# Alternating the two column ranges of 768-column products inside each k-tile

## The chip, the cores and the metric

One Trainium2 chip, and one of its NeuronCores. The metric is the device time of one execution in microseconds; below a time is a median of several runs unless it is called the profiled execution, which is one run with the hardware profiler on.

## What is computed

Two blocks of a small diffusion-like network in float32, with d = 1024, 256 context tokens and 512 latent tokens. The first block has a hybrid layer and an attention layer, each followed by an MLP; the second has two gated layers on the latent tokens alone.

```python
hx = rms_norm(x, norm1_g[layer]) * (1 + mod_x[1]) + mod_x[0]
hc = rms_norm(s_c, norm1_g[layer]) * (1 + mod_c[1]) + mod_c[0]
y_c, y_x = hybrid_mixer(hc, hx, ...)        # layer 0: projections (h @ w_in), mLSTM, gated conv, @ w_out
...                                         # layer 1: attention_mixer
x = x + mod_x[2] * y_x
x = x + mod_x[5] * sqrelu_mlp(rms_norm(x, ...) * (1 + mod_x[4]) + mod_x[3], mlp_w1[layer], mlp_w2[layer])
# layer 0 does the same for the context tokens s_c
```

All large products have the form weights times activations, with activations held transposed: channels on the 128 partitions, tokens along the free dimension. In layer 0 and in the keys and values of layer 1 the weights apply to context and latent tokens together, 256 + 512 = 768 columns. Everything later is on the 512 latent columns.

## The kernel before

Weights come in units of 1024 x 128 (512 KB), one for each tile of 128 output channels. SyncE loads unit t into slot t % 4 of Wraw, ScalarE copies it to Whi in float32r, and VectorE makes Wlo = Wraw - Whi. Activations too are kept as a high and a low part (h_hi, h_lo; hid_hi, hid_lo; mixa, mixb, mixc in the same way). A product is then the sum of three matmul passes for each k-tile of 128 input channels: Whi with hi, Whi with lo, Wlo with hi. KD = 8 k-tiles make one output tile, accumulated in PSUM.

`product(t, src, rng, ...)` (lines 547 to 563) computes one output tile. It waits for w_lo (the split weights) and for tile_free of its PSUM tensor, issues all passes, and counts tile_done with its last pass. `parts(rng)` (line 335) cuts the token range: FULL, 768 columns, gives (0, 256) and (256, 768); LAT, the 512 latent columns, gives one part. `ps(G[t % 2], a, b)` is where a part goes in PSUM: columns 256 to 512 of G for the 256-column part and 512 to 1024 for the other, thus two banks of 512 floats. G[0] and G[1] alternate from tile to tile, so that ScalarE and VectorE read one tile while TensorE writes the next; both wait for tile_done before they read either part.

Every `pe.matmul` is two instructions on the chip: LDWEIGHTS puts 128 weight columns into the array (PEld in the profile) and MATMUL streams 256 or 512 columns of activations past them (PE).

`product` is used with FULL by the hybrid layer's projections (units 2 to 24), by its output projection (4 tiles), by the MLP of layer 0 and by two tiles of the attention's keys and values; with LAT by everything behind that. The first two tiles of a group are made by others. `first_products` (line 565) runs two tiles at once, a k-tile of one and then a k-tile of the other a few behind, with all three passes of 256 and then all three of 512 in each (lines 587 to 589). `full_part` (line 742 to 744) and `part_product` (654 to 656) make one part of a tile at the seams between groups, where a norm is still being computed for the other part.

Line numbers are those of the kernel before.

Of the kernel before, what the change touches and what calls it, by code (L numbers as in the profile page):

```python
# [14 lines left out]
P = 128  # L15
# [84 lines left out]
def wait(eng, sem, at):  # L100

    if not isinstance(at, At):
        at = At(at)
    if at.positive():
        eng.wait_ge(sem, at.value())


def build(nc, xin, cvec, wstream, adaw, firstw, vecs_d, consts_d, rope_d, poolw_d, sguw_d, rows_d, out):
    ctx = ExitStack()
    with ctx:  # L110
        def sb(name, shape, dt=F32, where=ctx):
            return where.enter_context(nc.sbuf_tensor(name, shape, dt))
# [13 lines left out]
        Wlo = sb("Wlo", [P, 4, D], F32R)  # L126
        Whi = sb("Whi", [P, 4, D], F32R)
# [141 lines left out]
        G = [ctx.enter_context(nc.psum_tensor(f"G{i}", [P, 1024], F32)) for i in range(2)]  # L269
# [8 lines left out]
        def ps(bank, a, b):  # L278

            return bank[:, NC + a:NC + b]  # L280
# [54 lines left out]
        def parts(rng):  # L335
            return [(0, NC), (NC, NT)] if rng == FULL else [(NC, NT)]
# [73 lines left out]
        def is_apart(t):  # L410

            return t.i is None and t.c in APART

        def w_of(t):

            if is_apart(t):
                n = APART[t.c][0]
                return Eraw[:, n, :], Ehi[:, n, :], Elo[:, n, :]
            return Wraw[:, t % 4, :], Whi[:, t % 4, :], Wlo[:, t % 4, :]
# [126 lines left out]
        def _(pe):  # L546
            def product(t, src, rng, kt=KD, from_group=False):

                wait(pe, w_lo, t + 1)
                wait(pe, tile_free[t % 2], t // 2 + (-1 if from_group else 0))  # L550
                s = t % 4
                for a, b in parts(rng):
                    for k in range(kt):
                        hi, lo = src(k)
                        if is_apart(t):
                            wh, wl = [w[:, k * P:(k + 1) * P] for w in w_of(t)[1:]]
                        else:
                            wh, wl = Whi[:, s, k * P:(k + 1) * P], Wlo[:, s, k * P:(k + 1) * P]
                        o = ps(G[t % 2], a, b)
                        pe.matmul(o, wh, hi[:, a:b], start=(k == 0), stop=False)  # L560
                        pe.matmul(o, wh, lo[:, a:b], start=False, stop=False)  # L561
                        last = pe.matmul(o, wl, hi[:, a:b], start=False, stop=(k == kt - 1))  # L562
                last.then_inc(tile_done, 1)

            def first_products(t, src, rng, sem, at, kt=KD, between=None, order=None, lag=None):
# [27 lines left out]
            def tiles(pair):  # L593

                return lambda k: (pair[0][:, k, :], pair[1][:, k, :])

            def latent(pair):

                class Shifted:
                    def __init__(self, ap):  # L600
                        self.ap = ap

                    def __getitem__(self, key):
                        return self.ap[:, key[1].start - NC:key[1].stop - NC]

                return lambda k: (Shifted(pair[0][:, k, :]), Shifted(pair[1][:, k, :]))
# [204 lines left out]
            def mlp(t0, h, hid, rng, sset, h0_, edge):  # L811
                src = tiles(h) if rng == FULL else latent(h)
                hsrc = tiles(hid) if rng == FULL else latent(hid)

                def chunk(i, c0):
                    u0, g0 = t0 + 2 * CH * c0, h0_ + CH * c0
                    if c0 == 0 and rng == FULL:
                        full_start(edge, u0, src)
                    elif c0 == 0:
                        edge_start(edge, u0, src, sset)  # L820
                    else:
                        first_products(At(u0, i, 2 * CH), src, rng, src_ready, At(8 * sset))
                    group = c0 == 0 and rng == LAT
                    for j in range(4 if group else 2, CH):
                        product(At(u0 + j, i, 2 * CH), src, rng, from_group=group and j < 6)
                    first_products(At(u0 + CH, i, 2 * CH), hsrc, rng, hid_ready, At(g0, i, CH))
                    split = rng == FULL and c0 == n - 1
                    for m in range(2, KD - 2 if split else KD):
                        product(At(u0 + CH + m, i, 2 * CH), hsrc, rng)
                    if split:  # L830
                        full_end(edge + 1, u0 + 2 * CH - 2, hsrc)

                n = HID // P // CH
                chunk(None, 0)
                with pe.Fori(0, n - 2 if rng == FULL else n - 1) as i:
                    chunk(i, 1)
                if rng == FULL:
                    chunk(None, n - 1)
# [35 lines left out]
            src = tiles(h0)  # L874
# [99 lines left out]
            for t in range(2, N_HYB):  # L974
                product(At(t), src, FULL)
                if t == 5:
                    gate_columns()
                if 6 <= t < 10:
                    turn(t - 6, 0, TT)
                if t == 7:  # L980
                    turn_keys(0)
                if t in (8, 9):
                    chunk_states(0, t - 8)
                if t in S_SLOT:
                    scores(S_SLOT.index(t))
                if t in A_SLOT:
                    spread_max(A_SLOT.index(t))
                if t in C_SLOT:
                    numerators(C_SLOT.index(t))
                if t == 12:  # L990
                    turn_keys(1)
                if t in (15, 16):
                    chunk_states(1, t - 15)
                if t >= 22:
                    turn_head(t - 22)
# [17 lines left out]
            src = tiles(h2)  # L1013
# [33 lines left out]
            for t in range(N_ATT):  # L1047
                rng = FULL if t < 4 else LAT
# [90 lines left out]
            src = latent(ao)  # L1139
# [6 lines left out]
            for l in range(2):  # L1146
                t0 = T_S + l * N_S
                src = latent(hs)
# [50 lines left out]
                src = latent(ms)  # L1199
# [5 lines left out]
                src, hsrc = latent(hs), latent(hid2)  # L1205

                for c0, n_up in ((0, CH), (1, CH), (2, NF - 2 * CH)):
                    t = t1 + 24 * c0
# [1836 lines left out]
```

## Time and profile before

| | |
|---|---|
| median of 3 runs | 2559.99 us |
| lowest and highest | 2555.70 and 2561.22 us |
| profiled execution, its own time | 2557.46 us |
| its span, first to last instruction | 2555.80 us |
| PE busy in the span | 2512.2 us, 98% |
| PEld busy | 2120.1 us, 83% |
| VectorE (DVE), ScalarE (ACT) busy | 1617.5 us, 63%; 970.0 us, 38% |
| mean granted TensorE clock | 0.993 of full |

The span is what the profile's rows cover. Busy time is a union over the instructions of an engine; the ends of matmuls are modelled, and successive ones overlap, so that the start of one to the start of the next is shorter than its duration.

### The profile page before, as it was taken

How to read it: one execution, taken by the hardware profiler on the slowest of the kernel's cores; microseconds unless marked ns; L12 is line 12 of the kernel's file. 1: busy time of each engine (PE TensorE's matmuls, PEld its weight loads, DVE VectorE, ACT ScalarE, POOL GpSimd, SP SyncE). 2: the span in 40 equal slices, each digit the busy share in tenths (PEclk: the TensorE clock that was granted, in tenths of full speed). 3: DMA queues.
4: the chain of work that ended last, by engine and by line, in shares of the span. 5: the costliest groups of instructions: out<-in, count | busy, mean ns of one | idle time of the engine just before them, and what ended most of it. 6: DMA issues, size and time to landing. Idle time of an engine off the chain costs nothing.

```text
span 2555.8 us, 36124 instructions
## 1 busy us (share of the span) xinstructions
PE 2512.2 (98%) x13956; PEld 2120.1 (83%) x13956; DVE 1617.5 (63%) x2547; ACT 970.0 (38%) x1440; POOL 93.8 (4%) x181
## 2 busy tenths in 40 slices
PE   8999999999999999999999999999999999999997
PEld 6888888888888886669888888888888888888887
DVE  5777666764646556666655566776667867744447
ACT  6243533131313244764332243453232454533234
POOL 0000000000000000000000000000001000000000
PEclk9999999999999999999999999999999999999998
DMA  7323413433333311002545553324456323132322
GB/s 284 109 98 100 140 50 132 165 116 116 115 107 130 110 67 50 1 1 83 198 149 170 175 189 112 107 100 162 159 173 221 117 95 108 67 99 92 98 99 91
DMA packets 83963, 303.68 MB, mean 119 GB/s; under 512 B 9200, under 2 KB 11376, under 8 KB 83568
## 3 DMA queue, kind: packets, MB, share of 16 engines
q1 hardware_dynamic: 58336, 208.92, 24.0%
q0 software_dynamic: 25488, 92.81, 10.7%
q8 instruction: 99, 1.62, 0.3%
q14 instruction: 40, 0.33, 0.0%
HBM read 299.60 MB, written 2.10 MB: 118 GB/s over the span
## 4 chain that ended last, share of the span: by engine, by line
PE 93%; DVE 4%; ACT 1%; DMA 1%; issue 1%; SPq 0%; DVEq 0%; ACTq 0%
PE G L560 20%; PE G L562 20%; PE G L561 20%; PE G L587 5%; PE G L589 5%; PE G L588 5%; PE B L1116 2%; PE G L654 1%; PE G L655 1%; PE G L656 1%; PE G L1078 1%; PE B L1092 1%; PE G L742 1%; PE G L744 1%; PE G L743 1%
## 5 line engine op out<-in xcount | busy, mean ns | idle before, releaser
L1233 ACT ACTIVATE Whi<-Wraw 128x1024 fp32r<-128x1024 f32 x335 | 351.6, 1051 | 412.6 <-DMA Wraw<-wstream_dram 401.2
L1841 DVE TENSOR_TENSOR Wlo<-Wraw,Whi 128x1024 fp32r<-128x1024 f32 x335 | 409.5, 1223 | 132.4 <-ACT Whi L1233 131.4
L560 PE MATMUL G<-h_hi,Whi 128*128 128x256 f32 (+1 forms) x1008 | 351.8, 349 | 0.6 <-ACT T L1354 0.3
L562 PE MATMUL G<-h_hi,Wlo 128*128 128x256 f32 (+1 forms) x1008 | 350.3, 348 | 0.0
L561 PE MATMUL G<-h_lo,Whi 128*128 128x256 f32 (+1 forms) x1008 | 349.5, 347 | 0.0
L562 PE MATMUL G<-hid_hi,Wlo 128*128 128x512 f32 (+1 forms) x760 | 276.6, 364 | 0.0
L560 PE MATMUL G<-hs_hi,Whi 128*128 128x512 f32 x688 | 271.9, 395 | 4.8 <-DVE Wlo L1841 3.8
L561 PE MATMUL G<-hid_lo,Whi 128*128 128x512 f32 (+1 forms) x760 | 276.3, 364 | 0.0
L560 PE MATMUL G<-hid_hi,Whi 128*128 128x512 f32 (+1 forms) x760 | 275.7, 363 | 0.0
L561 PE MATMUL G<-hs_lo,Whi 128*128 128x512 f32 x688 | 268.9, 391 | 0.0
L562 PE MATMUL G<-hs_hi,Wlo 128*128 128x512 f32 x688 | 268.9, 391 | 0.0
L1856 DVE SCALAR_TENSOR_TENSOR Araw<-Araw,CB 128x1024 f32<-128x1024 f32 x176 | 214.3, 1220 | 12.4 <-DMA Araw<-adaw_dram 12.3
L560 PEld LDWEIGHTS G<-h_hi,Whi 128*128 128x128 f32 x1008 | 189.3, 188 | 27.3 <-issue 2.8
L561 PEld LDWEIGHTS G<-h_lo,Whi 128*128 128x128 f32 x1008 | 189.3, 188 | 24.6
L562 PEld LDWEIGHTS G<-h_hi,Wlo 128*128 128x128 f32 x1008 | 189.3, 188 | 24.4
L1916 DVE SCALAR_TENSOR_TENSOR X<-G,MOD,X 128x256 f32<-128x256 f32 (+1 forms) x104 | 65.2, 656 | 203.7 <-PE G L562 151.8
L561 PEld LDWEIGHTS G<-hid_lo,Whi 128*128 128x128 f32 x760 | 142.6, 188 | 23.6
L560 PEld LDWEIGHTS G<-hid_hi,Whi 128*128 128x128 f32 x760 | 142.6, 188 | 23.6 <-issue 0.3
L527 POOL DMA_DIRECT2D Araw<-adaw_dram x176 | 93.1, 529 | 1871.7 <-DVE Araw L1856 1817.1
L562 PEld LDWEIGHTS G<-hid_hi,Wlo 128*128 128x128 f32 x760 | 142.7, 188 | 22.4
L560 PEld LDWEIGHTS G<-hs_hi,Whi 128*128 128x128 f32 x688 | 129.9, 189 | 33.5 <-DVE Wlo L1841 5.8
L561 PEld LDWEIGHTS G<-hs_lo,Whi 128*128 128x128 f32 x688 | 129.9, 189 | 27.4 <-issue 1.0
(521 smaller groups left out, 4701.4 us busy)
## 6 DMA issues: line engine op xcount, KB each, us to landing
Wraw<-wstream_dram SPq DMA_DIRECT2D x335, 512.0 KB, 3.3
Araw<-adaw_dram POOLq DMA_DIRECT2D x176, 512.0 KB, 3.8
Eraw<-wstream_dram SPq DMA_DIRECT2D x22, 512.0 KB, 4.4
FIRST<-firstw_dram SPq DMA_DIRECT2D x6, 1024.0 KB, 19.5
X<-xin_dram SPq DMA_DIRECT2D x4, 768.0 KB, 7.0
X<-xin_dram SPq DMA_DIRECT2D x2, 1536.0 KB, 7.7
out_dram<-X SPq DMA_DIRECT2D x16, 128.0 KB, 1.7
ROW<-rows_dram SPq DMA_DIRECT2D x2, 768.0 KB, 6.7
```

The source lines that it names most:

```text
L527: pool.dma_start(Araw[:, n % 2, :], adaw[bass.ds(n.value(), 1), :, :].rearrange("a p n -> p (a n)") if n.i is not None else adaw[n.c]).the ...
L560: pe.matmul(o, wh, hi[:, a:b], start=(k == 0), stop=False)
L561: pe.matmul(o, wh, lo[:, a:b], start=False, stop=False)
L562: last = pe.matmul(o, wl, hi[:, a:b], start=False, stop=(k == kt - 1))
L587: pe.matmul(o, wh, hi[:, a:b], start=(nth == 0), stop=False)
L588: pe.matmul(o, wh, lo[:, a:b], start=False, stop=False)
L589: last = pe.matmul(o, wl, hi[:, a:b], start=False, stop=(nth == kt - 1))
L1116: last = pe.matmul(B6[HD * e:HD * (e + 1), 512 + 2 * P * half:512 + 2 * P * (half + 1)], AV[:, i, g * HD:(g + 1) * HD], PT[:, r % 2, TT * ...
L1233: act.activation(hi, raw, ACT.Copy).then_inc(w_hi, 1)
L1841: dve.tensor_tensor(lo, raw, hi.bitcast(F32), ALU.subtract).then_inc(w_lo, 1)
L1856: last = dve.scalar_tensor_tensor(out=products, in0=Araw[:, n % 2, :], scalar=1.0, in1=CB[:, v, :], op0=ALU.mult, op1=ALU.mult, accum_out=o)
L1916: last = dve.scalar_tensor_tensor(out=X[:, m, a:b], in0=ps(G[t % 2], a, b), scalar=MOD[:, par, v, gate * 8 + m:gate * 8 + m + 1], in1=X[:, ...
```

## The change

In `product`, the loop over parts moves from outside the loop over k-tiles to inside, and within a k-tile also inside the loop over the three pairs of weights and activations. For a 768-column tile the passes of one k-tile are then (Whi, hi, 256), (Whi, hi, 512), (Whi, lo, 256), (Whi, lo, 512), (Wlo, hi, 256), (Wlo, hi, 512). Each part's accumulation starts with its first pass at k = 0 and stops with its last at k = kt - 1. For a 512-column tile the order of passes is the one it had.

```diff
                 s = t % 4
-                for a, b in parts(rng):
-                    for k in range(kt):
-                        hi, lo = src(k)
-                        if is_apart(t):
-                            wh, wl = [w[:, k * P:(k + 1) * P] for w in w_of(t)[1:]]
-                        else:
-                            wh, wl = Whi[:, s, k * P:(k + 1) * P], Wlo[:, s, k * P:(k + 1) * P]
-                        o = ps(G[t % 2], a, b)
-                        pe.matmul(o, wh, hi[:, a:b], start=(k == 0), stop=False)
-                        pe.matmul(o, wh, lo[:, a:b], start=False, stop=False)
-                        last = pe.matmul(o, wl, hi[:, a:b], start=False, stop=(k == kt - 1))
+                for k in range(kt):
+                    hi, lo = src(k)
+                    if is_apart(t):
+                        wh, wl = [w[:, k * P:(k + 1) * P] for w in w_of(t)[1:]]
+                    else:
+                        wh, wl = Whi[:, s, k * P:(k + 1) * P], Wlo[:, s, k * P:(k + 1) * P]
+                    for n, (w, x) in enumerate(((wh, hi), (wh, lo), (wl, hi))):
+                        for a, b in parts(rng):
+                            last = pe.matmul(ps(G[t % 2], a, b), w, x[:, a:b], start=(k == 0 and n == 0),
+                                             stop=(k == kt - 1 and n == 2))
                 last.then_inc(tile_done, 1)
```

## Rows read from the trace of the kernel before

**Rows 1.** The page's totals by engine, and its chain that ended last by engine.
```profile
PE 2512.2 (98%) x13956; PEld 2120.1 (83%) x13956; DVE 1617.5 (63%) x2547; ACT 970.0 (38%) x1440; POOL 93.8 (4%) x181
...
PE 93%; DVE 4%; ACT 1%; DMA 1%; issue 1%; SPq 0%; DVEq 0%; ACTq 0%
```

**Rows 2.** The page's costliest groups: busy us, mean ns of one, idle before.
```profile
L561 PE MATMUL G<-h_lo,Whi 128*128 128x256 f32 (+1 forms) x1008 | 349.5, 347 | 0.0
...
L561 PEld LDWEIGHTS G<-h_lo,Whi 128*128 128x128 f32 x1008 | 189.3, 188 | 24.6
```

**Rows 3.** Timeline of TensorE, one MLP tile: start us, us, instruction.
```profile
450.29 0.28 PE L560 MATMUL G<-hid_hi,Whi 128*128 128x256 f32 x1
...
453.01 0.39 PE L560 MATMUL G<-hid_hi,Whi 128*128 128x512 f32 x1
...
458.50 0.28 PE L560 MATMUL G<-hid_hi,Whi 128*128 128x256 f32 x1
```

**Rows 4.** Groups by form on PE, 384 to 878 us (layer 0's MLP).
```profile
L562 PE MATMUL G<-h_hi,Wlo 128*128 128x512 f32 x192 | 75.6, 394 | 0.0
L561 PE MATMUL G<-h_lo,Whi 128*128 128x512 f32 x192 | 75.3, 392 | 0.0
L560 PE MATMUL G<-h_hi,Whi 128*128 128x512 f32 x192 | 74.5, 388 | 0.0
...
L560 PE MATMUL G<-h_hi,Whi 128*128 128x256 f32 x192 | 53.1, 276 | 0.3 <-ACT T L1354 0.3
...
L560 PE MATMUL G<-hid_hi,Whi 128*128 128x256 f32 x176 | 48.6, 276 | 0.0
```

**Rows 5.** Groups by form on PE, the whole span: a 128-column matmul.
```profile
L1092 PE MATMUL G<-CON,PR 128*128 128x128 f32 x176 | 22.9, 273 | 1.0 <-ACT PR L1716 1.0
```

**Rows 6.** Groups by form on PE, 52 to 285 us (hybrid projections).
```profile
L561 PE MATMUL G<-h_lo,Whi 128*128 128x256 f32 x183 | 51.0, 279 | 0.0
```

**Rows 7.** Groups by form on PE, 44 to 51 us (first_products there).
```profile
L587 PE MATMUL G<-h_hi,Whi 128*128 128x512 f32 x7 | 2.8, 397 | 0.0
...
L589 PE MATMUL G<-h_hi,Wlo 128*128 128x512 f32 x7 | 2.7, 392 | 0.0
L587 PE MATMUL G<-h_hi,Whi 128*128 128x256 f32 x7 | 2.0, 282 | 0.0
L588 PE MATMUL G<-h_lo,Whi 128*128 128x256 f32 x7 | 2.0, 280 | 0.0
```

**Rows 8.** Timeline of TensorE in single-range stages, around 1250 and 1170 us.
```profile
1249.99 0.39 PE L587 MATMUL G<-hid_hi,Whi 128*128 128x512 f32 x1
...
1251.35 0.39 PE L560 MATMUL G<-hid_hi,Whi 128*128 128x512 f32 x1
...
1169.72 0.28 PE L655 MATMUL G<-ao_lo,Ehi 128*128 128x256 f32 x1
...
1170.80 0.28 PE L655 MATMUL G<-ao_lo,Ehi 128*128 128x256 f32 x1
```

**Rows 9.** Groups by form on PE, the whole span: 256-column passes with h.
```profile
L560 PE MATMUL G<-h_hi,Whi 128*128 128x256 f32 x392 | 110.9, 283 | 0.3 <-ACT T L1354 0.3
```

**Rows 10.** Groups by form on PE, 312 to 345 us (output projection).
```profile
L560 PE MATMUL G<-mixa_hi,Whi 128*128 128x256 f32 x16 | 4.4, 276 | 0.0
```

**Rows 11.** Timeline of TensorE, one tile of the hybrid projections.
```profile
60.98 0.28 PE L560 MATMUL G<-h_hi,Whi 128*128 128x256 f32 x1
...
69.31 0.28 PE L560 MATMUL G<-h_hi,Whi 128*128 128x256 f32 x1
```

**Rows 12.** Timeline of TensorE, `first_products` in the MLP, three groups.
```profile
565.27 0.28 PE L587 MATMUL G<-hid_hi,Whi 128*128 128x256 f32 x1
...
568.35 0.28 PE L587 MATMUL G<-hid_hi,Whi 128*128 128x256 f32 x1
```

**Rows 13.** Timeline of TensorE, `first_products` ahead of the projections, four groups.
```profile
45.27 0.28 PE L587 MATMUL G<-h_hi,Whi 128*128 128x256 f32 x1
...
49.48 0.28 PE L587 MATMUL G<-h_hi,Whi 128*128 128x256 f32 x1
```

## Prediction

> **What bounds the kernel now.** I read the totals and the chain of work first. TensorE's matmul row is busy for 2512.2 of 2555.8 us and 93% of the chain that ended last is matmuls [rows 1]. So anything that changes the pace of the matmuls moves the end, and almost nothing else does. A matmul here is a *pass*: 128 weight columns stay in the array and 256 or 512 columns stream past them. The groups of instructions show a second fact: lines 560 and 561 use the same weights Whi one after the other, and yet each has as many weight loads as matmuls, 1008 and 1008 [rows 2]. A repeat of the weights saves no load.
>
> Busy times of a matmul overlap, because their ends are modelled, so durations don't add up. What adds up is the spacing between starts, which the timeline gives. Inside a tile of the MLP the 24 passes of 256 columns run from 450.29 to 453.01 us, 113.3 ns each, and the 24 of 512 from 453.01 to 458.50, 228.8 ns each [rows 3]. Over the whole MLP of the first layer (384 to 878 us) the durations are 276 ns for 256 columns and 388, 392 and 394 ns for the three 512-column passes of a k-tile [rows 4]; 276 less 113 is 163, and 163 less from the others gives 225, 229 and 231 ns, whose mean is again 228.5. So a duration minus 163 ns is a spacing, and with that the grouped rows can be read to the nanosecond.
>
> Three things in them matter. The spacing is nearly proportional to columns, so passes are bound by streaming. It is not wholly so: a 128-column pass of line 1092 has 273 ns, thus 110 ns of spacing [rows 5], so a load and a pass cannot follow faster than about 110 ns, and a 256-column pass has only some 3 ns of room above that. And passes of one size don't have one price. In the hybrid layer's projections 256-column passes have 279 ns (116) [rows 6], in the first products there 280 to 282, and 392 to 397 for 512 columns [rows 7]; in the single-range stages 512 columns cost 226.7 ns (six passes from 1249.99 to 1251.35) and elsewhere 256 columns cost 120 ns (nine from 1169.72 to 1170.80) [rows 8]. The chip has several paces for the same pass, and stays in one for many passes.
>
> **The change, part by part.** It removes nothing and adds nothing: each k-tile of a 768-column tile has three passes of 256 and three of 512 columns before and after, each with its own load, from the same addresses into the same two PSUM ranges. The waits ahead of a tile and the count behind it are where they were, on the same last pass (wl, hi, 512 columns, last k). Nobody reads the 256-column half earlier, because ScalarE and VectorE both wait for tile_done. No DMA, no queue and no order of another engine is touched. Single-range tiles (512 columns) have one part and stay as they are, and so do `first_products`, `full_part` and `part_product`.
>
> How many passes are moved: of 768-column tiles in `product` the by-form rows have 392 / 8 = 49 with h [rows 9] and 176 / 8 = 22 with hid [rows 4]; the mix sources have 16 k-tiles with mixa [rows 10] and, in two more such rows, 8 with mixb and 8 with mixc, together 32, thus 4 tiles. Together 75 tiles, 1800 pairs of a 256- and a 512-column pass. Of those, 50 tiles lie in the even pace (4 with mix [rows 10], 192 / 8 = 24 with h and 22 with hid [rows 4]) and 25 in the slower pace of the projections of the two mixers.
>
> The price of a pair today: in the even pace 8.21 us / 24 = 342.1 ns [rows 3]. In the slower one a tile runs from 60.98 to 69.31 us, 8.33 / 24 = 347.1 ns [rows 11].
>
> What the change alters is only the neighbours. Before, a tile has one step from 256 to 512 and one back; after, 24 and 24, and each step is also a change of the PSUM bank. The trace has this half way: `first_products` runs three passes of 256, then three of 512, then three of 256 of the other tile. In the even pace three such groups take 565.27 to 568.35 us, 3.08 us for nine pairs, 342.2 ns [rows 12]: eight times as many steps of size as in the block order, and no cost or gain. In the slow pace four groups run from 45.27 to 49.48 us, 4.21 us for twelve pairs, 350.8 ns [rows 13], against 347.1 in blocks. So there mixing costs 3.7 ns a pair.
>
> The loads: the load for the next pass starts with the present one, so before the change 24 loads of a tile lie under a 256-column pass and 24 under a 512-column pass, and after it the same. The room of 3 ns under the short pass is no smaller. I cost this at nothing; its cover is those 3 ns, and what it costs without them is in the bounds.
>
> Sum for the forecast: even pace 0 x 1200 pairs; slow pace 3.7 ns x 600 = +2.2 us. Against the profiled execution of 2557.46 us (span 2555.80 and 1.66 around it) that is 2559.7. The median of the three runs is 2559.99, 2.5 above the profiled one, so the median forecast is 2562.
>
> Bounds of what no row shows, a 256-column pass directly after a single 512-column one. Below: the short pass stays at 113.3 and the long one takes the 225 ns of the first 512-column pass behind short ones (388 less 163 [rows 4]), 338.3 ns a pair: 3.8 x 1200 + 8.8 x 600 = 4.6 + 5.3 = -9.9 us. Above: the slow mixed pace everywhere, 8.7 x 1200 + 3.7 x 600 = 10.4 + 2.2 = +12.7 us; with the dearest rows of each size, 120 [rows 8] and 397 less 163 = 234 [rows 7], 354 ns, it is 11.9 x 1200 + 6.9 x 600 = +18.4 us. I take the value of the rows nearest in kind, the mixed loops [rows 12, 13], which are real interleaved streams with the same operands.
>
> The Trainium skill, "TensorE: Matmul & The Clock Gate", section "Back-to-back issue gap", gives a warm gap of N / 2.4 + 2.5 ns, whatever stands before. By it a pair would cost 109 + 216 = 325 ns in either order, and the change nothing. The order part agrees with the even rows; the size does not (342 measured), and the slow rows show a dependence on neighbours that the rule lacks.
>
> **Rivals.**
> *The slow mixed pace spreads (slower).* The alternation puts every 256-column pass behind a 512-column one. In the even pace the three 512-column passes of a k-tile cost 225, 229 and 231 ns in that fixed turn [rows 4], and in all mixed code of that pace the short ones follow the 231 one. With the change two of three follow a 225 or 229 one. In the slow mixed loop the 512-column pass ahead of the short ones is the one of 392 ns, thus 229 [rows 7], and what follows is slow. That speaks for it; against it speaks that the even loop holds for over 400 us [rows 4, 10]. Place: all 50 even tiles. Price: +12.7 us, thus 2573 as a median. It decides from 5.1 us / 1800 = 2.8 ns a pair.
> *Each long pass takes the cheap 225 ns (faster).* For it: the first long pass behind short ones is always the cheap one in the even pace. Against it: the three differ around one mean, as if what the first saves the next pays back. Price: -9.9 us, 2550.
> *Loads get cheaper.* The order puts two passes on each load's weights, four on Whi. The Trainium skill, same page, section "Step-by-step: what each phase is for", says that loading and multiplying are apart so that weights can be loaded once and used by several matmuls. If such loads cost nothing, passes would run at the undisturbed 113.3 + 226.7 = 340 ns: 2.1 x 1200 + 7.1 x 600 = -6.8 us, 2553. Against it: 1008 loads for 1008 matmuls on equal weights in a row [rows 2].
> *The change does nothing at all*, not even in the slow pace: 2560. It lies within the forecast's class.
>
> **How the numbers follow.** A measurement of this kernel can tell about 0.2%, 5.1 us, from no change. No measurable change (forecast and "nothing at all"): 0.50. The slow pace spreads, fully or over 2.8 ns a pair: 0.37. Cheap long passes: 0.10; cheaper loads: 0.03. So faster 0.13, same 0.50, slower 0.37. The predicted time is the likeliest case, 2562 us, its own range 2557 to 2566. The 8-in-10 range takes in the spread slow pace and two thirds of the gain: 2552 to 2575.
>
> **What would show it.** In the timeline of an MLP tile: six passes of a k-tile in 1.03 us and a tile in 8.21 us if I am right; 1.05 us and 8.42 if the slow pace spread; 1.015 or less if the long passes became cheap. By form, durations of 256 columns near 276 ns (right) or 280 to 283 (slow pace). The number of loads stays 13956. No new wait of TensorE on another engine. In the hybrid projections a tile of 8.42 in place of 8.33 us. The prediction is wrong if the mean spacing of a pair in the MLP moves by more than 2.8 ns either way.

## The result and the profile after

The changed kernel takes 2576.62 us (four runs, 2573.72 to 2577.38) against 2560.59 us (four runs, 2555.70 to 2561.22) before: ratio 1.0057, 95% interval 1.0039 to 1.0076. That is slower by more than 0.2%, and 1.6 us beyond the top of the predicted range. The profiled execution has a span of 2572.1 us, 16.3 more than before.

The totals and the chain by engine, as [rows 1]:

```profile
PE 2528.7 (98%) x13956; PEld 2130.3 (83%) x13956; DVE 1617.0 (63%) x2547; ACT 970.0 (38%) x1440; POOL 93.8 (4%) x181
...
PE 92%; DVE 4%; ACT 1%; DMA 1%; issue 1%; SPq 0%; POOL 0%; POOLq 0%; DVEq 0%; ACTq 0%
```

There are as many matmuls and as many loads as before, and TensorE's longest waits are still on the same producers (6.1 us for the input, 4.2 us for Wlo). Busy time grew by 16.5 us on TensorE, and by 10.2 on its weight loads, and on no other engine: the same instructions follow each other more slowly.

Groups by form on PE, 384 to 878 us, the hid tiles, as [rows 4]:

```profile
L560 PE MATMUL G<-hid_lo,Whi 128*128 128x512 f32 x158 | 62.9, 398 | 0.0
L560 PE MATMUL G<-hid_hi,Whi 128*128 128x512 f32 x158 | 62.7, 397 | 0.0
L560 PE MATMUL G<-hid_hi,Wlo 128*128 128x512 f32 x158 | 61.9, 392 | 0.0
L560 PE MATMUL G<-hid_lo,Whi 128*128 128x256 f32 x158 | 45.0, 285 | 0.0
L560 PE MATMUL G<-hid_hi,Wlo 128*128 128x256 f32 x158 | 44.6, 282 | 0.0
L560 PE MATMUL G<-hid_hi,Whi 128*128 128x256 f32 x159 | 44.4, 279 | 0.0
```

Less 163 ns, the short passes are spaced 122, 119 and 116 ns (113 in [rows 4]) and the long ones 235, 234 and 229 (229, 225 and 231 there). The timeline of TensorE gives the sum. Two passes of one pair of operands are merged in it as x2:

```profile
49.83 0.28 PE L586 MATMUL G<-h_hi,Whi 128*128 128x256 f32 x1
...
52.91 0.50 PE L560 MATMUL G<-h_hi,Whi 128*128 128x256 f32 x2
...
61.38 0.51 PE L560 MATMUL G<-h_hi,Whi 128*128 128x256 f32 x2
...
69.86 0.51 PE L560 MATMUL G<-h_hi,Whi 128*128 128x256 f32 x2
...
441.36 0.28 PE L586 MATMUL G<-hid_hi,Whi 128*128 128x256 f32 x1
...
458.00 0.52 PE L560 MATMUL G<-hid_hi,Whi 128*128 128x256 f32 x2
...
508.88 0.28 PE L586 MATMUL G<-h_hi,Whi 128*128 128x256 f32 x1
```

From 458.00 to 508.88 lie six tiles of `product`: 50.88 us / 144 pairs = 353.3 ns, against 342.1 in [rows 3]. A tile of the hybrid projections has 69.86 - 61.38 = 8.48 us, 353.3 ns a pair too, against 347.1 in [rows 11]. So `product` has one pace now in both stages, 1060 ns for the six passes of a k-tile. It is there from the first tile: ahead of it `first_products` ran three groups from 49.83 to 52.91 us, 342.2 ns a pair, the even pace, and eight k-tiles of the alternation then take 8.47 us (52.91 to 61.38). And `first_products` in the MLP, whose code is unchanged, takes 16.64 us from 441.36 to 458.00, where it took 16.43 (433.86 to 450.29): it starts out of the even pace, right behind an alternating tile, and doesn't come back to it.

The stages side by side. The columns are: stretch, its us, busy time and count of PE, PEld, DVE, ACT and POOL, granted clock, DMA share, GB/s. The four stretches are the hybrid layer, its output projection, the MLP of layer 0, and the rest. Before:

```profile
30.73:291.61 260.88, 260.88 (x1687) 226.85 (x1683) 187.38 (x326) 112.71 (x220) 13.32 (x25) 1.00 0.35 121
291.61:362.27 70.66, 67.72 (x401) 59.48 (x400) 37.74 (x60) 23.42 (x32) 0.53 (x1) 1.00 0.27 90
362.27:894.74 532.47, 529.83 (x3098) 464.95 (x3096) 327.07 (x468) 134.28 (x156) 30.07 (x57) 1.00 0.35 120
894.74:2555.80 1661.06, 1630.16 (x8629) 1355.86 (x8627) 1049.11 (x1671) 680.95 (x999) 49.70 (x94) 0.99 0.34 115
```

After:

```profile
31.25:296.37 265.12, 265.12 (x1686) 229.96 (x1683) 187.34 (x326) 112.64 (x220) 13.32 (x25) 0.99 0.35 118
296.37:368.16 71.79, 69.00 (x402) 60.31 (x400) 37.58 (x59) 23.35 (x32) 0.53 (x1) 1.00 0.25 89
368.16:914.61 546.45, 543.81 (x3098) 474.13 (x3097) 327.42 (x468) 134.32 (x156) 30.07 (x57) 1.00 0.35 117
914.61:2572.10 1657.49, 1626.53 (x8629) 1352.64 (x8627) 1048.31 (x1671) 681.07 (x999) 49.71 (x94) 0.99 0.34 115
```

The MLP gives 13.98 of the 16.3 us: 46 tiles x 24 pairs x 11.2 ns = 12.4, and seven calls of `first_products` x 0.21 = 1.5. The output projection gives 1.13 (4 x 24 x 11.2 ns = 1.08). The hybrid layer gives 4.24: 23 tiles x 24 x 6.2 ns = 3.4, and a stretch near 89 us at the lower clock, which is why that row has 0.99; how much of the remainder is due to it isn't worked out. Behind the MLP the code is the same but for the two tiles of keys and values, and it was 3.57 us shorter in this execution (for about its last third the granted clock was 0.98 before and 0.99 after); the start was 0.52 us later. For the 16.3 us the granted clock isn't the cause: in the MLP it is 1.00 in both.

### The profile page after: what moved, and what is told of

It is laid out like the page before. It is cut to its first block, busy times and chain, and to the rows that moved or that the text cites. A ratio compares the mean times of both kernels' runs of the same rounds, so it can differ in the third digit from the quotient of the medians.

```text
span 2572.1 us, 36124 instructions
## 1 busy us (share of the span) xinstructions
PE 2528.7 (98%) x13956; PEld 2130.3 (83%) x13956; DVE 1617.0 (63%) x2547; ACT 970.0 (38%) x1440; POOL 93.8 (4%) x181
## 4 chain that ended last, share of the span: by engine, by line
PE 92%; DVE 4%; ACT 1%; DMA 1%; issue 1%; SPq 0%; POOL 0%; POOLq 0%; DVEq 0%; ACTq 0%
PE G L560 60%; PE G L586 5%; PE G L587 5%; PE G L588 5%; PE B L1115 2%; PE G L653 1%; PE G L655 1%; PE G L654 1%; PE G L1077 1%; PE B L1091 1%; PE G L741 1%; PE G L743 1%; PE G L742 1%; DMA FIRST<-firstw_dram 1%; PE G L1091 1%
## 5 line engine op out<-in xcount | busy, mean ns | idle before, releaser
L560 PE MATMUL G<-h_hi,Whi 128*128 128x256 f32 (+1 forms) x1008 | 292.3, 353 | 0.6 <-ACT T L1353 0.3
L560 PE MATMUL G<-h_lo,Whi 128*128 128x256 f32 (+1 forms) x1008 | 290.7, 351 | 0.0
L560 PE MATMUL G<-h_hi,Wlo 128*128 128x256 f32 (+1 forms) x1008 | 288.7, 350 | 0.0
L560 PE MATMUL G<-hid_lo,Whi 128*128 128x512 f32 (+1 forms) x760 | 250.5, 367 | 0.0
L560 PE MATMUL G<-hid_hi,Whi 128*128 128x512 f32 (+1 forms) x760 | 249.4, 366 | 0.4 <-DVE X L2899 0.4
L560 PE MATMUL G<-hid_hi,Wlo 128*128 128x512 f32 (+1 forms) x760 | 248.6, 365 | 0.0
L1855 DVE SCALAR_TENSOR_TENSOR Araw<-Araw,CB 128x1024 f32<-128x1024 f32 x176 | 214.0, 1219 | 12.8 <-DMA Araw<-adaw_dram 12.7
```

Of the source, the lines that this page charges most:

```text
L560: last = pe.matmul(ps(G[t % 2], a, b), w, x[:, a:b], start=(k == 0 and n == 0), stop=(k == kt - 1 and n == 2))
L1855: last = dve.scalar_tensor_tensor(out=products, in0=Araw[:, n % 2, :], scalar=1.0, in1=CB[:, v, :], op0=ALU.mult, op1=ALU.mult, accum_out=o)
```

## The experiments

All kernels below change only the order or the cut of the passes in `product`, or the place of buffers; one, banks_turn_same_columns, also leaves out part of the columns. Single times are from one run, beside one run or several of the kernel before on the same chip; such a time can be some 5 us off (the kernel before had 2559.65 and, as before_again, 2563.26 us side by side). What is compared is the pace in the MLP stage (and, where it matters how a stage was entered, in others): the MLP has granted clock 1.00 in all its rows shown below, and in the kernel before, before_again and all_shifted it took 532.47, 532.46 and 532.48 us. For 368 k-tiles of `product` in it, 1 us is 2.7 ns a k-tile. "Short" is 256 columns, "long" 512.

### First: how often must the size change?

Three short and three long passes for each k-tile (k_groups), and the alternation with the long pass ahead (long_first):

```diff
# k_groups, against the changed kernel
-                    for n, (w, x) in enumerate(((wh, hi), (wh, lo), (wl, hi))):
-                        for a, b in parts(rng):
...
+                    for a, b in parts(rng):
+                        o = ps(G[t % 2], a, b)
+                        pe.matmul(o, wh, hi[:, a:b], start=(k == 0), stop=False)
...
# long_first, against the changed kernel
-                        for a, b in parts(rng):
+                        for a, b in parts(rng)[::-1]:
```

> In each k-tile three passes of 256 columns, then three of 512 (the order of first_products), in product. Theory A (what costs is a short pass right behind a lone long one): the short ones follow the third long one, so a k-tile in the MLP stays at 1.03 us and the time within 5 us of before, 2556 to 2565 us. Theory B (every step to the other part costs, whatever stands around it: the PSUM bank or the size): 8 steps back a tile in place of 24, so a third of the added 16 us, 2566 us, and 1.04 us a k-tile.

> The changed kernel with the 512-column pass of each pair first. Theory A and theory B: the same turn of short and long but for the tile's ends, so 2572 to 2580 us and 353 ns a pair. If the order within the pair matters (the short pass after a long one on the same weights is the dear one, or on new weights): back under 2568 us.

k_groups: 2562.80 us (10 runs) against 2564.96 (21), ratio 0.9987, interval 0.9977 to 0.9997, less than the 0.2% that the prediction took as measurable. Its timeline of TensorE:

```profile
52.57 0.28 PE L560 MATMUL G<-h_hi,Whi 128*128 128x256 f32 x1
...
53.60 0.28 PE L560 MATMUL G<-h_hi,Whi 128*128 128x256 f32 x1
...
320.14 0.28 PE L560 MATMUL G<-mixc_hi,Whi 128*128 128x256 f32 x1
...
321.19 0.28 PE L560 MATMUL G<-mixb_hi,Whi 128*128 128x256 f32 x1
```

and one of its groups in the MLP:

```profile
L560 PE MATMUL G<-hid_hi,Whi 128*128 128x256 f32 x166 | 46.3, 279 | 0.0
```

The same code runs at 1.03 us a k-tile at 52.57, at 1.05 at 320.14, and in the MLP in a third way: the short passes have 279 and 280 ns, where [rows 4] has 276. Their starts are 118 ns apart there. (For such passes a duration less 163 ns gives 116 or 117, thus 1 to 2 ns too little.) The MLP stage took 539.07 us; 6.6 us more over the 480 k-tiles of `product` and `first_products` are 13.8 ns each, so 1.040 us a k-tile. Each pace holds for many tiles on end, the first for the four tiles from 52.57 to 85 us, the second for the four of the output projection, the third for the whole MLP: this order keeps the pace in which it is entered. The 342.2 ns of [rows 12] were the pace of the block tiles ahead, carried on, and not a price of mixing.

long_first: 2576.01 us (4 runs), ratio 1.0044, interval 1.0027 to 1.0060, forms 398, 397, 392 and 285, 282, 279 ns: the same three and three as in the changed kernel. Which size leads makes no difference.

### Second: is it the size, or the alternation?

All passes of 256 columns, in blocks (thirds_block), or the first two ranges in turn (thirds_turn). Both have 1800 more passes, and loads, in place of long ones.

```diff
# thirds_block
-                for a, b in parts(rng):
+                cut = [(0, NC), (NC, 2 * NC), (2 * NC, NT)] if rng == FULL else [rng]
+                for a, b in cut:
# thirds_turn
+                cuts = [[(0, NC), (NC, 2 * NC)], [(2 * NC, NT)]] if rng == FULL else [[rng]]
+                for cut in cuts:
                     for k in range(kt):
...
+                        for n, (w, x) in enumerate(((wh, hi), (wh, lo), (wl, hi))):
+                            for a, b in cut:
```

> product cuts 768 columns in three parts of 256, all passes of one part first; 9 passes a k-tile in place of 6. Passes keep the even pace of 113.3 ns: 1.02 us a k-tile, 6.7 ns less than before over 600 k-tiles, so 2556 us. If they fall to 118 or 120 ns (short passes on other columns): 1.06 to 1.08 us a k-tile, +20 to +32 us, 2580 to 2592 us.

> As thirds_block, but the first two parts (all 256 columns, in the two PSUM banks) take turns pass by pass, as in the change; sizes are equal. Theory A in the form that unequal sizes side by side are the cause: the same time as thirds_block within 5 us. Theory B in the form that the turn of banks or of activations' columns is the cause: slower than thirds_block by 5 us or more, with 118 ns or more a pass in the turned part.

thirds_block took 2576.18 us (6 runs), ratio 1.0049 (1.0031 to 1.0067), thirds_turn 2576.37 (10 runs), ratio 1.0027 (1.0007 to 1.0047): the same median within 0.2 us, with single runs from 2562 to 2584. Groups in the MLP, of thirds_block:

```profile
L561 PE MATMUL G<-hid_hi,Whi 128*128 128x256 f32 x507 | 139.9, 276 | 0.0
```

and of thirds_turn:

```profile
L562 PE MATMUL G<-hid_hi,Whi 128*128 128x256 f32 x458 | 103.2, 279 | 0.0
```

So in the MLP the turn has the slower spacing (118 ns by the starts) and the block has 113. In the output projection it is the other way round. The starts of two tiles of 72 passes, by the timeline of TensorE, of thirds_turn:

```profile
328.53 0.39 PE L562 MATMUL G<-mixa_hi,Whi 128*128 128x256 f32 x2
...
336.69 0.28 PE L562 MATMUL G<-mixa_hi,Whi 128*128 128x256 f32 x1
```

and of thirds_block:

```profile
325.28 0.28 PE L561 MATMUL G<-mixa_hi,Whi 128*128 128x256 f32 x1
...
333.76 0.28 PE L561 MATMUL G<-mixa_hi,Whi 128*128 128x256 f32 x1
```

The turn takes 8.16 us / 72 = 113.3 ns a pass, the block 8.48 / 72 = 117.8. Equal passes thus have either spacing in either order, and keep the one in which the stage is entered. Alternation alone, without unequal sizes, takes nothing from the even pace: at 330 us, 48 of the 72 passes of a tile change bank and columns from each to the next, at 113.3 ns throughout. The changed kernel entered its first tile in the even pace too, and lost it at once. So the size is part of the cause. That the MLP is entered at 118 ns by thirds_turn and k_groups, and at 113 by thirds_block and the kernel before, isn't explained; each is one trace, and whether the turn has a part in how a stage is entered stays open.

### Third: banks, columns, or where the operands lie?

The alternation changes the PSUM bank and the columns with each pass. banks_turn_same_columns changes only the bank (its second part reads the first 256 columns again and leaves out columns 256 to 512). one_bank_turn changes only the columns, for the 512-column part; it keeps one long pass at the start and one at the end of that part. And 192 bytes put behind Whi change only the distance between the tensors up to Whi, the weights among them, and those behind it, the activations among them:

```diff
# banks_turn_same_columns, against thirds_turn
+                                r = (0, NC) if len(cut) == 2 else (a, b)
# one_bank_turn: 512-column part, but for its first and last pass
+                            halves = rng == FULL and a == NC and not start and not stop
+                            for c, d in [(NC, 2 * NC), (2 * NC, NT)] if halves else [(a, b)]:
# block_aligned (order as before), turn_aligned (order as changed)
         Whi = sb("Whi", [P, 4, D], F32R)
+        sb("shift_line", [P, 48])
```

> thirds_turn with both turning parts reading the first 256 columns of the activations (the second part's product is then that of the wrong tokens), so only the PSUM bank turns. If the turn of PSUM banks is the cause: 118 ns a pass in the MLP, as in thirds_turn. If the turn of activation columns is: 113.3 ns. If it is the pairs of passes on equal weights, 118 ns here and in one_bank_turn.

> Block order, but the 512-column part is issued as two 256-column passes in turn, both in one PSUM bank (its first and last pass of a tile stay whole). If the turn of banks is the cause: 113.3 ns a pass, as in thirds_block. If the turn of activation columns or the pairs on equal weights are: 118 ns.

> The kernel before with 192 bytes of empty space behind Whi, which moves every later tensor: the 768-column activations now start at the same residue modulo 512 bytes as the weights (128), and those of the 512-column stages lose it (128 becomes 320). Theory C (the pace is set by where a pass reads its activations relative to where its neighbour's weights are read): passes of 512 columns in the MLP go to 226.7 ns all three, and those of 512 in the later stages leave 226.7 ns. Theory D (only the order of passes and what went before set the pace): 1.027 us a k-tile in the MLP and 226.7 ns later, as before; time within 5 us of before.

> The same 192 bytes in the changed kernel. Theory C: the pace of a pair no longer depends on the turn, so 353 ns falls and the kernel takes the same as block_aligned within 5 us. Theory D: 353 ns a pair and 16 us above block_aligned.

banks_turn_same_columns: 2577.02 us, 279 and 280 ns in the MLP. one_bank_turn: 2586.95 us, 279 and 280 ns. Read alone, these rows would say that either turn costs 5 ns a pass; but as in thirds_turn, what the stage was entered with is in them. Where banks_turn_same_columns was entered in the even pace, it stays there, in the first tiles of the hybrid projections as in the output projection. One tile of 72 passes, 8.16 us, 113.3 ns each:

```profile
60.61 0.39 PE L563 MATMUL G<-h_hi,Whi 128*128 128x256 f32 x2
...
68.77 0.39 PE L563 MATMUL G<-h_hi,Whi 128*128 128x256 f32 x2
```

A turn of the bank costs nothing there. And one_bank_turn shows the step at which a pace is lost, in its first tile:

```profile
52.76 0.28 PE L563 MATMUL G<-h_hi,Whi 128*128 128x256 f32 x1
...
55.48 0.39 PE L563 MATMUL G<-h_hi,Whi 128*128 128x512 f32 x1
55.70 0.40 PE L563 MATMUL G<-h_lo,Whi 128*128 128x256 f32 x2
...
60.89 0.40 PE L563 MATMUL G<-h_hi,Wlo 128*128 128x512 f32 x1
```

24 short passes take 2.72 us, 113.3 each. Then comes a single long one of 0.22, and the 44 short ones behind it take 5.19 us, 118 each. One lone long pass took the short ones out of the even pace, and nothing in 44 of them brought it back. These 44 turn their columns too; but thirds_turn turned columns and bank together at 113.3, so the long pass is what is left.

block_aligned: 2596.80 us (4 runs) against 2558.31 (7), ratio 1.0146 (1.0119 to 1.0173). turn_aligned: 2605.26 (4), ratio 1.0180 (1.0153 to 1.0206). Not one instruction differs between block_aligned and the kernel before but for addresses, and it costs 38 us (2596.80 less 2558.31). turn_aligned is 8.5 us above block_aligned, between what the two theories said (5 or less, and 16). Theory C had said that the long passes leave 226.7 ns in the later stages, and they did; that those of the MLP go to it, and they didn't. Groups of block_aligned in the MLP:

```profile
L561 PE MATMUL G<-hid_hi,Whi 128*128 128x512 f32 x165 | 64.5, 391 | 0.0
...
L561 PE MATMUL G<-hid_hi,Whi 128*128 128x256 f32 x168 | 47.4, 282 | 0.0
```

Short passes now cost about 120 ns even in blocks, and further on (1250 to 1543 us) the long ones have

```profile
L561 PE MATMUL G<-hid_hi,Whi 128*128 128x512 f32 x161 | 63.7, 396 | 0.0
```

thus 233 ns against the 226.7 of [rows 8]. Most of the 38 us come from there: behind the MLP it takes 1687.7 us (906.57 to 2594.3) where the kernel before takes 1661.06.

### Fourth: the neighbours, pass by pass

runs_2_4 has three short passes always, and in turn two and four long ones. turn_other_weights alternates, but in the six passes of a k-tile it has equal weights in a row once, where the changed kernel has them four times; block_other_weights takes them out of the block order altogether. before_again is the kernel before.

```diff
# runs_2_4
+                    for _ in range(kt // 2):
+                        for long in (2, 4):
+                            todo += [(0, *work[0].pop(0)) for _ in range(3)]
+                            todo += [(1, *work[1].pop(0)) for _ in range(long)]
...
# turn_other_weights
+                    turns = [(0, hh), (1, lh), (0, hl), (1, hh), (0, lh), (1, hl)] if rng == FULL else [
...
# block_other_weights
-                        pe.matmul(o, wh, lo[:, a:b], start=False, stop=False)
-                        last = pe.matmul(o, wl, hi[:, a:b], start=False, stop=(k == kt - 1))
+                        pe.matmul(o, wl, hi[:, a:b], start=False, stop=False)
+                        last = pe.matmul(o, wh, lo[:, a:b], start=False, stop=(k == kt - 1))
```

> product in runs of three short passes (256 columns), then two long ones (512), three short, four long. As many steps between the parts as k_groups (3 and 3), only the lengths of the long runs differ. Theory P (phase: in the even pace three long passes in a row bring the pace back to where a short pass is cheap, and one or two leave it elsewhere; 225, 229, 231 ns): the even pace can't hold, short runs after the two long ones cost 118 ns, the MLP is over 1.045 us a k-tile. Theory S (each step costs, whatever the runs): as k_groups, 1.027 to 1.040 us.

> The changed kernel's turn of one short and one long pass, but the two no longer share their weights: Whi-hi short, Wlo-hi long, Whi-lo short, Whi-hi long, Wlo-hi short, Whi-lo long. Theory W (the repeated load of equal weights is what is slow): the pace comes back, 1.027 to 1.040 us a k-tile in the MLP. Theory P (the lone long pass is): 1.060 us as in the changed kernel.

> The kernel before with the order Whi-hi, Wlo-hi, Whi-lo in each k-tile, so that no two passes in a row of a k-tile have equal weights. Theory W: faster than before, 226.7 ns long passes and 1.020 us a k-tile in the MLP, some 5 us in all. Theory P: the paces of before, 1.027 us if the MLP is entered in the even pace and up to 1.053 if not.

> The kernel before once more. If the pace of a stage depends on what went before it (a wait of another length), a second execution may run a stage at another pace of the same set: the MLP at 1.027 or 1.053 us a k-tile, the hybrid projections at 1.027 to 1.067. If order alone sets it: the same 1.0267 us in the MLP and the same paces everywhere to 0.5 ns.

runs_2_4 took 2560.11 us, and 1.040 us a k-tile in the MLP, as k_groups. That is at the top of what theory S allowed and below what theory P said; but the steps don't all cost alike, as theory S had it. Its timeline in the MLP, from the end of a run of four long passes on:

```profile
535.80 0.39 PE L569 MATMUL G<-h_hi,Wlo 128*128 128x512 f32 x1
536.04 0.28 PE L569 MATMUL G<-h_hi,Whi 128*128 128x256 f32 x1
...
536.38 0.39 PE L569 MATMUL G<-h_hi,Whi 128*128 128x512 f32 x1
...
536.83 0.28 PE L569 MATMUL G<-h_hi,Whi 128*128 128x256 f32 x1
...
537.07 0.51 PE L569 MATMUL G<-h_hi,Wlo 128*128 128x256 f32 x2
```

Behind four long passes the three short ones take 0.34 us (536.04 to 536.38), 113 each; behind two long ones the first two take 0.24 (536.83 to 537.07), about 120 each. (The two kinds of run also differ in whether the long pass ahead of them has Wlo or Whi; but block_other_weights below changes that and has the spacings of before.) So something is carried from pass to pass, and the long passes change it. In these orders one (one_bank_turn) or two long passes behind short ones in the even pace leave the next short ones at 118 to 120 ns; three (k_groups in its first tiles) or 24 (the kernel before) leave them as they were; and four more behind the two bring 113 back. In the changed kernel a short pass has one long one behind it and one ahead of it, and never gets back to 113.

turn_other_weights took 2572.65 us, with 398, 397, 392 and 285, 282, 279 ns in the MLP, as the changed kernel. With one step of equal weights a k-tile in place of four, the price is the same, so such steps are not the cause. In its first tiles, entered in the slow pace (52.51 us), it has another pace, 8.38 us a tile (60.88 to 69.26), 349.2 ns a pair: the alternation too isn't wholly free of how it is entered. block_other_weights took 2551.95 us beside 2559.65, but has 276 and 388, 392, 394 ns, exactly [rows 4]: no pace gained. Its mean granted clock was 0.997 beside 0.994, and one run shows no gain.

before_again took 2563.26 us. It has the MLP at the pace of before, but not the output projection, where the kernel before has 276 ns [rows 10]:

```profile
L560 PE MATMUL G<-mixa_hi,Whi 128*128 128x256 f32 x16 | 4.5, 280 | 0.0
```

It is the same kernel, so the order of passes doesn't by itself fix the pace of a stage: a second execution, perhaps on another chip, entered this one differently.

### Fifth: how far apart?

192 bytes ahead of all weights, so that weights and activations move together (all_shifted), and 64 and 448 bytes between them:

```diff
# all_shifted
         X = sb("X", [P, KD, NT])
+        sb("shift_line", [P, 48])
# block_shift_64 (n = 16), block_shift_448 (n = 112), turn_shift_64 (n = 16, order as changed)
         Whi = sb("Whi", [P, 4, D], F32R)
+        sb("shift_line", [P, n])
```

> The kernel before with the 192 empty bytes ahead of Wlo, so that weights and activations move by the same amount (Whi and Wlo from residue 128 to 320 modulo 512, the activations as in block_aligned). If the pace hangs on the distance of the activations from the weights: the paces of before, 1.027 us a k-tile in the MLP and 226.7 ns in the later stages. If it hangs on where the activations lie by themselves: the paces of block_aligned, 120 and 226.7 ns in the MLP and 233.3 ns later.

> The kernel before with 64 empty bytes behind Whi: the distance of the 768-column activations from the weights modulo 512 bytes goes from 320 to 384, that of the 512-column ones from 0 to 64. If the distance sets the pace, both move: some new pace between 113.3 and 120 ns (256 columns) and 226.7 and 236 ns (512), likely dearer in the later stages, so 2560 to 2600 us. If only the exact match at 0 matters: 1.027 us in the MLP as before.

> 448 empty bytes behind Whi: distances 256 and 448. As block_shift_64, a further point of the same curve: the MLP between 1.020 and 1.060 us a k-tile, the later stages dearer than at distance 0.

> The changed kernel with the 64 bytes of block_shift_64. If a short and a long pass in turn lock at 353 ns whatever the distance: 1.060 us a k-tile in the MLP, as at distances 320 and 0. If the lock belongs to the distance: another pace, below 1.055 us or above 1.065.

They took 2558.04, 2582.82, 2593.79 and 2587.12 us, beside 2565.83. The MLP stage by windows, columns as above. all_shifted:

```profile
364.09:896.57 532.48, 529.83 (x3098) 464.93 (x3097) 327.09 (x468) 134.21 (x156) 30.21 (x57) 1.00 0.35 120
```

block_aligned:

```profile
365.36:906.57 541.21, 538.60 (x3098) 474.37 (x3096) 327.50 (x468) 134.29 (x156) 30.21 (x57) 1.00 0.35 118
```

turn_aligned:

```profile
369.80:917.46 547.66, 545.05 (x3098) 473.01 (x3097) 327.39 (x468) 134.21 (x156) 30.21 (x57) 1.00 0.35 116
```

block_shift_64:

```profile
368.00:914.29 546.29, 543.69 (x3098) 474.01 (x3097) 327.44 (x468) 134.31 (x156) 30.21 (x57) 1.00 0.35 117
```

turn_shift_64:

```profile
368.82:914.58 545.76, 543.16 (x3097) 474.61 (x3096) 327.45 (x468) 134.28 (x156) 30.21 (x57) 1.00 0.34 117
```

Three things follow. Moved together, weights and activations run in the MLP as before, to 0.01 us: not the place counts but the distance between what lies ahead of the space and what lies behind it. 192 and 448 bytes, which differ by 256, give the same MLP stage to the hundredth (541.21 and 541.21 us) and the same forms (391, 391, 389 and 283, 283, 282). And what the alternation costs in the MLP depends on that distance. At the kernel's own it is 546.45 - 532.47 = 13.98 us; with 192 bytes more 547.66 - 541.21 = 6.45; with 64 more 545.76 - 546.29 = -0.53, nothing. What moves with the distance is mostly the block order, 532.47 to 546.29 us; the alternation stays within 545.76 to 547.66. At this kernel's own distance the block order has a fast pace to lose, with 64 bytes more it has none.

## Why the prediction was wrong

*What bounds the kernel, and that nothing is added.* Right: TensorE has 92% of the chain, the loads stayed at 13956, no new wait, all of the time in the spacing of the passes. That a duration less 163 ns is a spacing held up too: the six forms of the MLP give 1055 ns against 1060 by the timeline, and before 1024 against 1027, 0.3 to 0.5% low. For single forms it is not good to the nanosecond, as the prediction had it: the short passes of 279 ns [rows 6], read there as 116, start 118 ns apart.

*"Even pace 0 x 1200 pairs".* This is the step that failed. It took the mixed loop's 342.2 ns [rows 12] as the price of an alternating pair. The true one is 353.3, +11.2 ns: 13.4 us over the 1200 pairs. k_groups shows why the row misled: six passes of three and three keep the pace that they are entered in, at 1.03, 1.04 and 1.05 us a k-tile in one kernel. [rows 12] stands behind block tiles, so it showed their pace and not its own. And three long passes in a row leave the even pace as it is, while a lone one takes it away (one_bank_turn, 113.3 ns ahead of it and 118 behind), so the row of three and three wasn't near in kind. The prediction noted that the chip stays in one pace for many passes, and didn't ask what this makes of a row taken as a price.

*"Slow pace 3.7 ns x 600".* The direction was right, the size too small: 8.48 in place of 8.33 us a tile is 6.2 ns, thus 3.7 us and not 2.2. Its rows were those of one execution: in the changed kernel the unchanged `first_products` ahead of the projections was in the even pace (342.2 ns a pair from 49.83 us on), where [rows 13] has 350.8. So neither the code nor the change sets the pace in which this stage is entered, and the term rests on how one execution entered it.

*The rival "the slow mixed pace spreads".* It had the mechanism, a long pass that leaves the next short one out of its fast place, and the durations that it asked for (280 to 283; measured 279, 282 and 285). Its price was 12.7 us. By its own count 11.2 x 1200 + 6.2 x 600 = 17.2 us, and 1.5 more in `first_products`, which the prediction called untouched: its code is, its pace isn't. The upper bound with the dearest rows of each size, 354 ns and +18.4 us, was in the text and was nearly right; the range stopped at 2575, 2 above the rival's 2573, and left it out. The medians differ by 16.0 us. That this is below 17.2 + 1.5 is no merit of the count: in the profiled executions the stages up to the MLP give 19.4, and the rest was 3.6 shorter for no reason that lies in the change. (At its lower end the range took in 8 of the 9.9 us of gain, four fifths and not two thirds.)

*The cheap rivals.* Refuted. The long passes became dearer (392 to 398 ns), and so did the short ones. Loads of equal weights aren't free: there are 13956 for 13956 matmuls, and with fewer equal weights in a row (turn_other_weights, block_other_weights) the spacings are the same. The room of 3 ns under a short pass, to which the prediction tied the loads, explains nothing that was seen: a short pass has 113 ns behind four long ones and 120 behind two, with a load of the same size beneath. The Trainium skill, "TensorE: Matmul & The Clock Gate", section "Back-to-back issue gap", gives the formula that the prediction used for an isolated matmul. These passes stand in a stream with their loads, and no pair took the 325 ns that it gives: they have 342.1 before and 353.3 after.

*What is shown of the cause, and what isn't.* Shown: the price is the spacing of the passes, and it comes from short and long ones in single turn, entered from the even pace (49.83 to 61.38 us). Equal passes in turn, of bank or of bank and columns, keep the even pace; one step of equal weights in a row in place of four changes nothing; a lone long pass ends the even pace (one_bank_turn, and by runs of passes runs_2_4). The pace of a float32r pass also depends on the distance between what lies ahead of Whi's end and what lies behind it in SBUF (all_shifted against block_aligned), and was the same at 192 and 448 bytes. Argued only: that it is the distance between activations and weights that counts, since other tensors move with them; that the stream of activations and the load of the next weights meet in SBUF; and that a pass starts early or late against the other's turn. The Trainium skill, "SBUF — State Buffer", section "A bandwidth-pool intuition that's wrong (but worth ruling out)", gives the weight load a second read port, independent of that of the moving operand. By that the distance between the two should cost nothing; here 192 bytes make 541.21 of 532.47 us, and the measurement decides. Which of the two reads waits no trace here shows. Not tried: other distances than four, the 256- and the 512-column parts moved apart from each other, and another distance for h alone. What sets the pace in which a stage is entered stays open too, and with it how much of a difference between two single traces is order and how much entry.

No version with more than one run beat both kernels: k_groups gains 0.13% (0.03 to 0.23), less than 0.2%.

## What to carry to other kernels

A row from a mixed loop is a price only if the loop would reach the same pace from any start; look at what ran ahead of it, and at a second place where it is entered otherwise. The same holds for an experiment: two orders that differ in one stage may only have entered it differently, so look for a stage where each was entered in the same pace. Where TensorE is the bound and no wait is left, a new order of passes (0.6% here) or a shifted buffer (1.5%) moves the time by itself; compare spacings by form before looking for a cause elsewhere. Code that a change doesn't touch isn't free of it, if the engine carries a pace into it.

## What the runs showed of the hardware that was not expected

- 192 bytes of unused SBUF between weights and activations cost 38 us of 2558 (ratio 1.0146), the same 192 bytes ahead of both none that can be seen in the MLP (532.48 against 532.47 us).
- The same passes in the same order have three paces in one execution (k_groups), and one stage of the same kernel has two in two executions (before and before_again, output projection). The trace shows no wait in any of them.
- One long pass among 68 short ones moved those behind it from 113.3 to 118 ns (one_bank_turn).
- The least spacings in a steady stream at full clock, 113.3 and 226.7 ns, are 17/16 of 256 and 512 columns at 2.4 GHz (106.7 and 213.3). At the lower level the sixteenth is gone. A stretch of before_again, by windows:

```profile
89.60:91.90 2.30, 2.30 (x11) 2.30 (x12) 0.00 (x0) 2.27 (x5) 0.00 (x0) 0.50 0.55 216
```

and two passes of it by the timeline, with four between them:

```profile
90.08 0.41 PE L562 MATMUL G<-h_hi,Wlo 128*128 128x256 f32 x1
...
91.14 0.41 PE L561 MATMUL G<-h_lo,Whi 128*128 128x256 f32 x1
```

The granted clock is 0.50, thus 1.2 GHz, and five spacings take 1.06 us, 212 ns each (213.3 for 256 columns at 1.2 GHz). In these passes, what slows one by a sixteenth or more at full clock costs nothing.
